# Mixing stage: the last prompt tile's branch products and the picks are placed behind the sample's last tile

## The chip, the cores and the metric

The kernel runs on one core of a Trainium2 chip. The metric is the device time of one execution in microseconds (us); smaller is better. An execution is one launch that computes both outputs, the prompt's 256 rows and the sample's 1024 rows.

## The reference

An encoder layer on two sequences of 256 and 1024 tokens, 1024 wide: input norm, one wide projection, neighbourhood attention (8 heads) beside a gated linear recurrence (4 heads, both directions), a gated mix of the two branches, a norm, and an expert-choice feed-forward layer with 16 experts. What the change touches is the mix, the router and the choice of tokens:

```python
a_out = a_out.reshape(B, T, NA_WIDTH) @ w_branch_na[l]
r_out = (o_hg * jax.nn.silu(g_hg)) @ w_branch_hg[l]
mix = jax.nn.sigmoid(gate_na) * a_out + jax.nn.sigmoid(gate_hg) * r_out
x = layer_norm(ALPHA * x + mix @ w_out[l], ln1_g[l], ln1_b[l])
...
cap = EC_FACTOR * n_tok // N_EXPERTS
aff = jax.nn.softmax((xf @ w_router).astype(jnp.float32), axis=-1)
gate, idx = lax.top_k(aff.T, cap)
xs = xf[idx]
hdn = jax.nn.silu(jnp.einsum('ecd,edf->ecf', xs, w_gate)) * jnp.einsum('ecd,edf->ecf', xs, w_up)
out = jnp.einsum('ecf,efd->ecd', hdn, w_down) * gate[..., None].astype(x.dtype)
```

Each expert takes its 32 best prompt tokens and its 128 best sample tokens. The whole layer runs once for the prompt and once for the sample.

## The kernel before

The kernel is one program of stages, written engine by engine: each engine (PE for matmuls, DVE, ACT, POOL, and SP, which issues loads) has its own instruction list in the order in which the code issues it, and semaphores join them. Nothing is scheduled by a tool: the order on each engine is the order of the calls. A stage ends at a barrier of all engines.

**The mixing stage** (`stage_mix_out`, L1504) works on 10 tiles of 128 tokens, in an order `MIX_ORDER` that takes the 8 sample tiles first (t = 0 to 7) and the 2 prompt tiles last (t = 8 and 9). For each tile t the steps, with the names that the code and this text use, are:

- `turn_oh`, `copy_oh`, `o_low`: the recurrence's normed output is transposed on PE (4 transposes, L1717), copied by ACT as the high part and split by DVE into its low part.
- `mix(t, x)`, x = 0, 1: the branch products, 24 matmuls of 512 columns for each half x of the output columns, 12 for each branch (L1736 to L1738); `weigh` (DVE, L2039) multiplies each by its gate, `add` (POOL, L1959) adds the two branches into `mixt`.
- `turn_mix`, `copy_mix`, `m_low`: 8 transposes on PE, the high part on ACT, the low part on DVE (L2045).
- `out(t, x)`: the output projection, 24 matmuls for each half (L1755 to L1757); `add_up` (DVE, L2053 and L2056) adds the residual and takes the statistics, `gather_stats`, `invert` (POOL), `centre` (L2066) and `shift` (L2076) do the norm.
- `turn_x1`, `copy_x1`, `logits`: 8 transposes and 8 small router products (L1770, 16 columns wide), then `find_max` (DVE, L2081), `exp` (ACT, L1894), `normalise` (DVE), `turn_aff` (one transpose on PE, L1775) and `keep` (DVE, L2104), which puts the tile's router weights into the table `affT`.

PSUM gives the transposes two buffers, `tp[0]` and `tp[1]`, used in turn in the order of the list `units`: a transpose waits (`wait_bank`) until the low part of the one two places ahead in that list has been taken. In a steady turn of the loop, PE does `turn_aff(t-2)`, `turn_oh(t+1)`, `mix(t+1, 0)`, `turn_mix(t)`, `mix(t+1, 1)`, `turn_x1(t-1)`, `out(t, 0)`, `logits(t-1)`, `out(t, 1)`.

**The picks.** DVE finds each expert's best tokens in rounds of three instructions over `affT` (`pick`, L1492: the 8 largest, their positions, their removal; L1498, L1500, L1501), so 47 picks for 128 tokens. As soon as the 8 sample tiles are in `affT`, the first `EARLY_PICKS` = 24 of them run on DVE in the mixing stage, in gaps between the work of tiles 8 and 9. The others run at the start of the expert stage. The prompt's rows of `affT` can take part only when tile 9 is in; its 4 rounds are the `JOINT_ROUNDS` 8 to 11, where one instruction works on sample rows and prompt rows together (80 rows and not 48).

**The start of the expert stage** (`stage_experts`, L2226). DVE: picks 24 to 35 (the joint ones), pick 36, `find_prompt`, pick 37, `list_prompt` (the prompt's lists, L2888 and on, which wait for a transpose on PE), picks 38 to 46, `list_sample` (writes `pair`, waits for PE to turn it, then writes the list of the sample's tokens, L2897 to L2916). POOL: gathers the prompt's rows once `list_prompt` is there and the sample's rows once `list_sample` is. PE, in this order: `turn_prompt_lists`, 28 transposes that keep it busy (`warm`, L2639), `turn_in_prompt` (the gathered prompt rows), then `session(0)`, 128 prompt products (L2559); the transposes of the sample's lists are called inside that session, ahead of its fourth piece of weights:

```python
for m in range(SESSION):
    g = SESSION * n + m
    if g == 3:
        turn_sample_lists()
    pe.wait_ge(w_ready[g % RAW], 16 * (g // RAW + 1))
```

Each piece has 16 products, so that 48 stand ahead of them. After the session come the sample's gathered rows, transposed and split, and then 16 experts' matmuls without a pause worth the name.

## Time and profile before

| | us |
|---|---|
| median of 3 runs | 2694.84 |
| lowest and highest run | 2692.8, 2696.47 |
| the profiled execution, its own time | 2697.44 |
| its span, first to last instruction | 2695.7 |

The profiled execution is 2.6 us above the median of the runs. PE is busy for 97% of the span, and TensorE's granted clock has a mean of 0.986 of full speed. In the rows further down, a line of a timeline or of the chain of waits begins with the start in us from the span's start and the duration in us; what stands in square brackets is the idle time of the engine ahead of it and what ended it. A count (x4) says that several instructions are merged. In the table by windows each engine has its busy time in us and its instructions; then come the granted clock of TensorE, the busy share of the DMA engines and GB/s. The length that a PE row shows includes its drain: from start to start the 512-column matmuls stand 0.23 us apart.

### The profile page before, as it was taken

To read this page: it belongs to the slowest core of one execution; us is meant where nothing else is said; L and a number is where in the kernel's file an instruction comes from. 1 tells how busy PE (TensorE), PEld (TensorE's weight loads), DVE (VectorE), ACT (ScalarE), POOL (GpSimd) and SP (SyncE) were. 2 spreads that over 40 slices of the span, in tenths; PEclk is the share of its full clock that TensorE was granted. 3 is DMA by queue.
4 is the path that set the end of the run, shared out by engine and by line. 5 is a ranking of instruction groups with operands and counts; after the bars stand their busy time and mean duration, and the time that the engine had idled before them with its cause. 6 is when DMAs were issued, how large, how long until landed. Compare 5 with 4: busy or idle time off the path is not lost.

```text
span 2695.7 us, 44888 instructions
## 1 busy us (share of the span) xinstructions
PE 2617.9 (97%) x18504; PEld 2079.8 (77%) x18504; DVE 1673.8 (62%) x2091; ACT 1370.4 (51%) x1800; POOL 507.0 (19%) x454
## 2 busy tenths in 40 slices
PE   9999999999999999969999999999999999999997
PEld 7888888777778788857777777777777777777775
DVE  7212220875654566576777667776777667776887
ACT  3111220866664434325566656665566656666674
POOL 2211120123332234310110010001001100111444
PEclk9999999999999999979999999999999999999999
DMA  7567783676666743366778877888788878888983
GB/s 252 172 197 211 242 276 125 240 292 215 215 239 225 257 156 125 118 244 237 281 289 294 313 276 282 293 313 290 267 304 303 289 286 304 301 286 329 342 337 128
DMA packets 238347, 683.59 MB, mean 254 GB/s; under 512 B 20081, under 2 KB 66680, under 8 KB 233024
## 3 DMA queue, kind: packets, MB, share of 16 engines
q1 hardware_dynamic: 220608, 630.58, 64.8%
q0 software_dynamic: 17536, 50.14, 6.6%
q8 instruction: 147, 2.41, 0.4%
q14 instruction: 56, 0.46, 0.0%
HBM read 576.67 MB, written 103.95 MB: 252 GB/s over the span
## 4 chain that ended last, share of the span: by engine, by line
PE 52%; DVE 1%; POOL 1%; issue 0%; ACT 0%; DMA 0%; ACTq 0%; POOLq 0%; DVEq 0%
PE moe_strip L2559 12%; PE moe_up L2574 4%; PE moe_down L2574 4%; PE moe_down L2576 4%; PE moe_up L2575 4%; PE moe_down L2575 4%; PE moe_up L2576 4%; PE moe_gate L2574 4%; PE moe_gate L2576 4%; PE moe_gate L2575 4%; PE moe_up L2496 1%; PE moe_turn L2532 1%; PE moe_gate L2507 0%; ACT pieces_high L2682 0%; POOL moe_minus_mean L2378 0%
## 5 line engine op out<-in xcount | busy, mean ns | idle before, releaser
L2790 DVE TENSOR_TENSOR pieces_low<-pieces_raw,pieces_high 128x1024 fp32r<-128x1024 f32 x768 | 893.6, 1219 | 349.9 <-PE moe_strip L2559 336.6
L2682 ACT ACTIVATE pieces_high<-pieces_raw 128x1024 fp32r<-128x1024 f32 x768 | 769.5, 1051 | 333.9 <-PE moe_up L2576 196.6
L2559 PE MATMUL moe_strip<-pieces_raw,pieces_xT_p 128*32 128x256 f32 x4096 | 227.9, 380 | 0.5 <-ACT pieces_xT_p L2694 0.5
L2574 PE MATMUL moe_gate<-pieces_high,pieces_xT 128*128 128x512 f32 x512 | 202.4, 395 | 1.5 <-DVE pieces_low L2790 0.8
L2574 PE MATMUL moe_up<-pieces_high,pieces_xT 128*128 128x512 f32 x512 | 202.9, 396 | 0.0
L2574 PE MATMUL moe_down<-pieces_high,pieces_hdn 128*128 128x512 f32 x512 | 202.8, 396 | 0.0
L2559 PEld LDWEIGHTS moe_strip<-pieces_raw,pieces_xT_p 128*32 128x32 f32 x4096 | 129.7, 110 | 93.8 <-issue 10.9
L2576 PE MATMUL moe_gate<-pieces_low,pieces_xT 128*128 128x512 f32 x512 | 199.6, 390 | 0.0
L2575 PE MATMUL moe_up<-pieces_high,pieces_xT 128*128 128x512 f32 x512 | 199.6, 390 | 0.0
L2575 PE MATMUL moe_gate<-pieces_high,pieces_xT 128*128 128x512 f32 x512 | 199.5, 390 | 0.0
L2576 PE MATMUL moe_down<-pieces_low,pieces_hdn 128*128 128x512 f32 x512 | 199.5, 390 | 0.0
L2575 PE MATMUL moe_down<-pieces_high,pieces_hdn 128*128 128x512 f32 x512 | 199.4, 389 | 0.0
L2576 PE MATMUL moe_up<-pieces_low,pieces_xT 128*128 128x512 f32 x512 | 199.1, 389 | 0.0
L2336 POOL COPY moe_at_in<-main_picks 32x1 uint32<-32x1 uint32 (+1 forms) x30 | 21.5, 744 | 768.9 <-PE moe_up L2496 764.3
L526 DVE COPY fr_out<-fr_acc 128x512 f32<-128x512 f32 (+1 forms) x28 | 17.7, 634 | 176.5 <-PE fr_acc L385 102.1
L1153 PE MATMUL hg_facc<-bias_fw,bias_fx 128*128 128x512 f32 x288 | 120.1, 417 | 5.6 <-PEq L103 2.1
L2574 PEld LDWEIGHTS moe_up<-pieces_high,pieces_xT 128*128 128x128 f32 x512 | 96.1, 188 | 32.3 <-issue 13.2
L2574 PEld LDWEIGHTS moe_down<-pieces_high,pieces_hdn 128*128 128x128 f32 x512 | 96.1, 188 | 25.8 <-issue 6.6
L1154 PE MATMUL hg_facc<-bias_fw,bias_fx 128*128 128x512 f32 x288 | 115.2, 400 | 0.0
L1155 PE MATMUL hg_facc<-bias_fw,bias_fx 128*128 128x512 f32 x288 | 114.9, 399 | 0.0
L2559 PE MATMUL moe_strip<-pieces_raw,moe_hdn_p 128*32 128x256 f32 x2048 | 113.8, 380 | 0.0
L2574 PEld LDWEIGHTS moe_gate<-pieces_high,pieces_xT 128*128 128x128 f32 x512 | 96.2, 188 | 21.8 <-DVE pieces_low L2790 1.9
(386 smaller groups left out, 5328.5 us busy)
## 6 DMA issues: line engine op xcount, KB each, us to landing
pieces_raw<-in_w_gate_e SPq DMA_DIRECT2D x128, 1024.0 KB, 5.3
pieces_raw<-in_w_up_e SPq DMA_DIRECT2D x128, 1024.0 KB, 7.3
pieces_raw<-in_w_down_e SPq DMA_DIRECT2D x128, 1024.0 KB, 5.0
bias_fx<-xs SPq DMA_DIRECT2D x40, 1024.0 KB, 5.3
fr_raw<-in_w_in SPq DMA_DIRECT2D x16, 1024.0 KB, 9.4
ws<-fr_late_split SPq DMA_DIRECT2D x32, 512.0 KB, 4.4
bias_fw<-ws SPq DMA_DIRECT2D x32, 512.0 KB, 9.0
mo_gates<-h SPq DMA_DIRECT2D x20, 512.0 KB, 4.4
```

The costliest lines, as they stand in the source:

```text
L1153: nc.tensor.matmul(f_acc[i % 2][:], fx[:, i % 2, 0, c, :], hi, start=(c == 0), stop=False)
L1154: nc.tensor.matmul(f_acc[i % 2][:], fx[:, i % 2, 0, c, :], lo, start=False, stop=False)
L1155: last = nc.tensor.matmul(f_acc[i % 2][:], fx[:, i % 2, 1, c, :], hi, start=False, stop=(c == KD - 1))
L2336: nc.gpsimd.tensor_copy(to[n][:], picks[n][:, e:e + 1]).then_inc(at_ready, 1)
L2496: last = nc.tensor.transpose(to[:, k * P:(k + 1) * P], rows_s[:, (4 * j + k) * P:(4 * j + k + 1) * P], ident[:])
L2532: last = nc.tensor.transpose(hidden_turned(c)[:, k * P:(k + 1) * P], hid[:, c % 2, k * P:(k + 1) * P], ident[:])
L2559: last = nc.tensor.matmul(strip_ps[j * CP:(j + 1) * CP, kind, :], x, raw[g % RAW][:, k * D + j * STRIP:k * D + (j + 1) * STRIP], start=sta ...
L2574: nc.tensor.matmul(to[:], x_k[:, kk, 0:CS], hi, start=(kk == 0), stop=False)
L2575: nc.tensor.matmul(to[:], x_k[:, kk, CS:2 * CS], hi, start=False, stop=False)
L2576: return nc.tensor.matmul(to[:], x_k[:, kk, 0:CS], lo, start=False, stop=(kk == count - 1))
L2682: nc.scalar.activation(high[:, g % HI, cols], raw[g % RAW][:, cols], ACT.Copy).then_inc(hi_done, 1)
L2790: nc.vector.tensor_tensor(low[g % RAW][:, cols], raw[g % RAW][:, cols], high[:, g % HI, cols].bitcast(F32), ALU.subtract).then_inc(lo_done, 1)
```

## The change

Only the mixing stage's orders and two constants are touched. The amount of work is the same: the same instructions run, with the same shapes, except that which pick stands in which stage changes. The steady loop now runs for t = 0 to 6, and from tile 7 (`Z`) on the order is written out for each engine. `mix(9, ...)`, the branch products of the last prompt tile, stand behind `logits(7)` and not ahead of `turn_x1(7)`. 33 picks run in the mixing stage in place of 24, and the joint rounds are 11 to 14 in place of 8 to 11, so that `find_prompt` and `list_prompt` follow picks 45 and 46, the last two. Nothing in `stage_experts` is edited.

```diff
-SAMPLE_TILES, EARLY_PICKS = SEQS[1][1] // P, 24
-JOINT_ROUNDS = range(8, 8 + CAPS[0] // 8)
+SAMPLE_TILES, EARLY_PICKS = SEQS[1][1] // P, 33
+JOINT_ROUNDS = range(11, 11 + CAPS[0] // 8)
...
+        units += [("mix", Z, 0), ("mix", Z, 1), ("oh", Z + 1, 0)]
+        units += [("x1", t, n) for t in (Z - 1, Z) for n in range(2)]
+        units += [("oh", Z + 2, 0)]
+        units += [(kind, t, n) for kind in ("mix", "x1") for t in (Z + 1, Z + 2) for n in range(2)]
...
+                turn_aff(Z - 2)
+                turn_mix(Z)
+                turn_oh(Z + 1)
+                mix(Z + 1, 0)
+                out(Z, 0)
+                turn_x1(Z - 1)
+                out(Z, 1)
+                logits(Z - 1)
+                mix(Z + 1, 1)
+                turn_aff(Z - 1)
+                turn_x1(Z)
+                turn_oh(Z + 2)
+                logits(Z)
+                mix(Z + 2, 0, (0,))
+                turn_aff(Z)
+                mix(Z + 2, 0, (1,))
+                turn_mix(Z + 1)
+                mix(Z + 2, 1)
+                out(Z + 1, 0)
+                out(Z + 1, 1)
+                turn_mix(Z + 2)
+                out(Z + 2, 0)
+                turn_x1(Z + 1)
+                out(Z + 2, 1)
+                logits(Z + 1)
+                turn_aff(Z + 1)
+                turn_x1(Z + 2)
+                logits(Z + 2)
+                turn_aff(Z + 2)
...
+                copy_x1(Z)
+                copy_oh(Z + 2)
+                open_gates(Z + 2, (0,))
+                exp(Z)
+                scale(Z)
+                open_gates(Z + 2, (1,))
...
+                invert(Z)
+                add(Z + 1, 1)
+                store(Z)
+                add(Z + 2, 0)
+                add(Z + 2, 1)
...
+                add_up(Z - 1, 1)
+                gather_stats(Z - 1)
+                m_low(Z)
+                o_low(Z + 1)
...
+                keep(Z)
+                pick_sample(0, 1)
...
+                pick_sample(12, 18)
+                add_up(Z + 1, 1)
+                gather_stats(Z + 1)
+                centre(Z + 1)
+                m_low(Z + 2)
+                shift(Z + 1)
+                pick_sample(18, 23)
+                add_up(Z + 2, 0)
+                pick_sample(23, 28)
+                find_max(Z + 1)
+                add_up(Z + 2, 1)
+                gather_stats(Z + 2)
+                centre(Z + 2)
+                normalise(Z + 1)
+                shift(Z + 2)
+                keep(Z + 1)
+                pick_sample(28, 31)
+                find_max(Z + 2)
+                pick_sample(31, 32)
+                normalise(Z + 2)
+                pick_sample(32, EARLY_PICKS)
+                keep(Z + 2)
```

The orders at three places follow, before and after. `mo_acc_out` is `out`'s accumulator, `mo_small` the router's, `mo_tp` the two transpose buffers, `mo_acc` the accumulators of `mix`.

PE where tile 7 begins, behind `out(6, 1)`, before:

```order
L1757 MATMUL mo_acc_out<-mo_wo_hi,mo_m_lo 128x512
L1775 MATMUL mo_small<-main_ident,mo_aff 80x128
L1717 MATMUL mo_tp<-main_ident,mo_oh 128x128 x4
L1736 MATMUL mo_acc<-mo_wb_hi,mo_act_hi 128x512
L1737 MATMUL mo_acc<-mo_wb_lo,mo_act_hi 128x512
```

and now:

```order
L1761 MATMUL mo_acc_out<-mo_wo_hi,mo_m_lo 128x512
L1779 MATMUL mo_small<-main_ident,mo_aff 80x128
L1723 MATMUL mo_tp<-main_ident,mo_mixt 128x128 x8
L1723 MATMUL mo_tp<-main_ident,mo_oh 128x128 x4
L1742 MATMUL mo_acc<-mo_wb_hi,mo_act_hi 128x512
```

The 8 transposes of `turn_mix(7)` moved from behind `mix(8, 0)` to ahead of `turn_oh(8)`, and fill both transpose buffers there.

DVE from the last picks ahead of `add_up(8, 1)` to `shift(8)`, before:

```order
L1498 MAX route_best<-main_affT 48x8
L1500 MAX_INDEX route_at<-route_best,main_affT 48x8
L2053 SCALAR_TENSOR_TENSOR wroom<-wroom,mo_acc_out 128x512
L2056 BN_STATS mo_stats<-wroom 128x6
L2060 BN_AGGR mo_mv<-mo_stats 128x2
L2045 TENSOR_TENSOR mo_m_lo<-mo_tp,mo_m_hi 128x512 x2
L2066 SCALAR_TENSOR_TENSOR wroom<-wroom,mo_mv,mo_g_all 128x1024
L2076 SCALAR_TENSOR_TENSOR wroom<-wroom,mo_rstd,mo_b_all 128x1024
```

and now:

```order
L1498 MAX route_best<-main_affT 48x8
L1500 MAX_INDEX route_at<-route_best,main_affT 48x8
L1501 MATCH_REPLACE main_affT<-route_best,main_affT 48x512
L2112 SCALAR_TENSOR_TENSOR wroom<-wroom,mo_acc_out 128x512
L2115 BN_STATS mo_stats<-wroom 128x6
L2119 BN_AGGR mo_mv<-mo_stats 128x2
L2125 SCALAR_TENSOR_TENSOR wroom<-wroom,mo_mv,mo_g_all 128x1024
L2104 TENSOR_TENSOR mo_m_lo<-mo_tp,mo_m_hi 128x512 x2
L2135 SCALAR_TENSOR_TENSOR wroom<-wroom,mo_rstd,mo_b_all 128x1024
```

`m_low(9)` moved behind `centre(8)`; six picks, not five, now stand between `add_up(8, 0)` and `add_up(8, 1)`.

DVE in the expert stage, from the second pick behind the joint ones, before:

```order
L1500 MAX_INDEX route_at<-route_best,main_affT 48x8
L2888 CAST moe_at_in<-moe_up 32x1
L2889 COPY main_gates<-moe_up 32x16
L2890 CAST main_picks<-moe_up 32x16
L2891 COPY main_gates<-moe_up 128x16
L2892 CAST main_picks<-moe_up 128x16
L1501 MATCH_REPLACE main_affT<-route_best,main_affT 48x512
L1498 MAX route_best<-main_affT 48x8
L1500 MAX_INDEX route_at<-route_best,main_affT 48x8
```

and now:

```order
L1500 MAX_INDEX route_at<-route_best,main_affT 48x8
L2968 CAST moe_at_in<-moe_up 32x1
L2969 COPY main_gates<-moe_up 32x16
L2970 CAST main_picks<-moe_up 32x16
L2971 COPY main_gates<-moe_up 128x16
L2972 CAST main_picks<-moe_up 128x16
L2977 COPY moe_pair<-route_best 16x128
L2978 TENSOR_SCALAR moe_pair<-route_at 16x128
```

The nine picks between `list_prompt` and the writing of `pair` are gone from there; ahead of them the same 14 picks stand as before.

## Rows read from the trace of the kernel before

**Rows 1.** Chain of waits, 1197 to 1240 us: start, us, what.

```profile
1209.15 5.07 PE moe_gate L2639 x28
...
1215.30 2.80 PE moe_strip L2559 x48
1218.09 0.27 PE moe_up L2633 x2
...
1219.45 4.30 DMA pieces_rows_s<-x,moe_at_in
...
1226.46 0.50 PE moe_gate L2574
```

**Rows 2.** Timeline of DVE, expert stage: start, us, engine, line, operation.

```profile
1197.85 0.69 DVE L1498 MAX8 route_best<-main_affT 80x8 f32<-80x512 f32 x1
...
1209.49 0.15 DVE L2888 CAST moe_at_in<-moe_up 32x1 uint32<-32x1 f32 x1
...
1217.27 0.21 DVE L2903 TENSOR_SCALAR moe_pair<-route_at 16x128 f32<-16x128 uint32 x1
1218.38 0.19 DVE L2906 COPY moe_taken<-moe_up 128x32 f32<-128x32 f32 x1 [0.90 <-PE moe_up L2633]
```

**Rows 3.** Windows: us; busy PE, PEld, DVE, ACT, POOL; PEclk; DMA.

```profile
1112.00:1138.00 26.00, 26.00 (x135) 21.95 (x134) 16.02 (x23) 9.92 (x14) 9.96 (x10) 1.00 0.32 101
...
1154.00:1159.00 5.00, 5.00 (x18) 4.02 (x19) 0.57 (x3) 0.52 (x3) 0.00 (x0) 0.66 0.96 354
...
1166.00:1175.00 9.00, 7.47 (x38) 6.10 (x37) 8.22 (x15) 2.15 (x3) 1.97 (x4) 1.00 1.03 411
...
1183.00:1187.00 4.00, 0.31 (x3) 0.21 (x2) 3.15 (x7) 0.58 (x3) 1.88 (x2) 0.83 0.00 0
1187.00:1193.00 6.00, 5.63 (x25) 5.23 (x25) 4.94 (x14) 2.04 (x3) 1.16 (x2) 0.50 0.44 175
```

**Rows 4.** Timeline of DVE, then PE, where tile 7 begins.

```profile
1112.97 0.69 DVE L2053 SCALAR_TENSOR_TENSOR wroom<-wroom,mo_acc_out 128x512 f32<-128x512 f32 x1 [4.56 <-PE mo_acc_out L1757]
...
1120.81 1.28 DVE L2045 TENSOR_TENSOR mo_m_lo<-mo_tp,mo_m_hi 128x512 fp32r<-128x512 f32 x2
...
1112.88 0.60 PE L1717 MATMUL mo_tp<-main_ident,mo_oh 128*128 128x128 f32 x4
...
1118.81 1.04 PE L1717 MATMUL mo_tp<-main_ident,mo_mixt 128*128 128x128 f32 x8
```

**Rows 5.** Timeline of DVE, then PE, around the second half of tile 8.

```profile
1161.85 0.69 DVE L2053 SCALAR_TENSOR_TENSOR wroom<-wroom,mo_acc_out 128x512 f32<-128x512 f32 x1 [0.25 <-PE mo_acc_out L1757]
...
1167.22 0.69 DVE L2053 SCALAR_TENSOR_TENSOR wroom<-wroom,mo_acc_out 128x512 f32<-128x512 f32 x1 [0.28 <-PE mo_acc_out L1757]
...
1168.80 1.23 DVE L2045 TENSOR_TENSOR mo_m_lo<-mo_tp,mo_m_hi 128x512 fp32r<-128x512 f32 x2
1169.95 1.27 DVE L2066 SCALAR_TENSOR_TENSOR wroom<-wroom,mo_mv,mo_g_all 128x1024 f32<-128x1024 f32 x1
...
1169.58 0.47 PE L1755 MATMUL mo_acc_out<-mo_wo_hi,mo_m_hi 128*128 128x512 f32 x1 [1.52 <-DVE mo_m_lo L2045]
```

**Rows 6.** Timeline of ACT in a tile of the steady loop.

```profile
1114.13 1.28 ACT L1868 ACT_TABLE_LOAD   x1
1115.42 2.01 ACT L1868 ACTIVATE mo_gates<-mo_gates 128x1024 f32<-128x1024 f32 x2
...
1133.57 0.28 ACT L1894 ACTIVATE mo_aff<-mo_small,mo_nmax 128x16 f32<-128x16 f32 x1 [5.41 <-DVE mo_nmax L2081]
```

**Rows 7.** Timeline of DVE, then PE, at the end of the mixing stage.

```profile
1185.47 1.28 DVE L2076 SCALAR_TENSOR_TENSOR wroom<-wroom,mo_rstd,mo_b_all 128x1024 f32<-128x1024 f32 x1 [0.75 <-issue]
...
1181.46 1.85 PE L1770 MATMUL mo_small<-mo_wr,wroom 128*128 128x16 f32 x16
1187.15 0.43 PE L1775 MATMUL mo_small<-main_ident,mo_aff 128*80 128x128 f32 x1 [3.84 <-DVE mo_aff L2087]
1187.38 1.92 PE L1717 MATMUL mo_tp<-main_ident,wroom 128*128 128x128 f32 x8
```

More of the change, by code:

```diff
@@ L1801, in _, with turn_mix, turn_x1 @@
                 mix(1, 0)
-                for t in range(0, NT + 2):
-                    if 0 <= t - 2 < NT and t - 2 != SAMPLE_TILES - 1:
+                def turn_mix(t):
+                    for n in range(2):
+                        pe.wait_ge(added, 2 * t + n + 1)
+                        turn(("mix", t, n), mixt[:, half_of(n)], m_turned)
+                def turn_x1(t):
+                    pe.wait_ge(x1_done, t + 1)
+                    for n in range(2):
+                        turn(("x1", t, n), x1_sb[:, half_of(n)], x1_turned)
@@ L1825, in _ @@
-                    if t == NT - 1:
-                        out(t, 1)
-                    if 0 <= t - 1 < NT and t != SAMPLE_TILES:
-                        logits(t - 1)
-                    if 0 <= t < NT - 1:
-                        out(t, 1)
+                    turn_mix(t)
+                    mix(t + 1, 1)
+                    if t >= 1:
+                        turn_x1(t - 1)
+                    out(t, 0)
+                    if t >= 1:
+                        logits(t - 1)
+                    out(t, 1)
@@ L1863, in copy_oh, with open_gates @@
                     nc.scalar.activation(act_hi[:, 1], blocks(bank_of(("oh", t, 0))[:]), ACT.Copy).then_inc(o_hi, 1)
-                def open_gates(t):
-                    for x in range(2):
+                def open_gates(t, halves=(0, 1)):
+                    for x in halves:
                         act.wait_ge(gates_in[x], 16 * t + 16)
@@ L2155, in _ @@
[L2155 to L2162 removed]
+                    weigh(t + 1, 1, 0)
+                    prepare(t + 2)
+                    weigh(t + 1, 1, 1)
+                    a_low(t + 2)
+                    norm_heads(t + 2)
@@ L2163, in _ @@
+                    add_up(t, 0)
+                    if t >= 1:
                         find_max(t - 1)
                         normalise(t - 1)
-                t = NT - 1
-                keep(t - 2)
-                pick_sample(0, 3)
-                add_up(t - 1, 0)
-                pick_sample(3, 8)
-                add_up(t - 1, 1)
-                gather_stats(t - 1)
-                m_low(t)
-                centre(t - 1)
-                shift(t - 1)
-                pick_sample(8, 11)
@@ L2177, in _ @@
-                add_up(t, 0)
-                pick_sample(11, 15)
-                add_up(t, 1)
-                gather_stats(t)
-                centre(t)
-                find_max(t - 1)
-                shift(t)
-                normalise(t - 1)
-                keep(t - 1)
-                pick_sample(15, 21)
-                find_max(t)
-                pick_sample(21, 22)
-                normalise(t)
-                pick_sample(22, EARLY_PICKS)
-                keep(t)
+                add_up(Z - 1, 1)
@@ new lines, in _ @@
+                gather_stats(Z - 1)
+                m_low(Z)
+                o_low(Z + 1)
+                centre(Z - 1)
+                keep(Z - 2)
+                shift(Z - 1)
+                weigh(Z + 1, 0, 0)
+                weigh(Z + 1, 0, 1)
+                prepare(Z + 2)
+                add_up(Z, 0)
+                norm_heads(Z + 2)
+                add_up(Z, 1)
+                gather_stats(Z)
+                find_max(Z - 1)
+                centre(Z)
+                normalise(Z - 1)
@@ new lines, in _ @@
+                shift(Z)
+                weigh(Z + 1, 1, 0)
+                weigh(Z + 1, 1, 1)
+                a_low(Z + 2)
+                keep(Z - 1)
+                o_low(Z + 2)
+                find_max(Z)
+                normalise(Z)
+                keep(Z)
+                pick_sample(0, 1)
+                weigh(Z + 2, 0, 0)
+                pick_sample(1, 2)
+                weigh(Z + 2, 0, 1)
+                m_low(Z + 1)
+                pick_sample(2, 5)
+                weigh(Z + 2, 1, 0)
```

120 lines of the change are left out of this document (55 added, 65 removed).

## The prediction, made before the changed kernel was run

> **What bounds the kernel now.** I read the windows first, then the timelines of the mixing stage's last tiles, then the chain of waits across the barrier. In the mixing stage's steady loop PE has no gap: 26.00 us busy in a window of 26.00 us, one tile, at the full clock, with DVE at 16.02 us [rows 3]. So up to tile 7 a step moved on DVE, ACT or POOL costs nothing, and the stage's length is PE's work plus what PE waits for. The places to look at are the waits of the tail, and those that the new order makes. Before, they are 1.52 us for `m_low(9)` [rows 5] and 3.84 us for tile 8's router weights [rows 7].
>
> Across the barrier the chain of waits does not run along the picks to their end. It runs from `list_prompt` to PE: the 28 keep-busy transposes (5.07 us), the prompt's gathered rows, 48 of the session's products (2.80 us), and only then, at 1218.09, the transposes of the sample's lists; from there to the gather of the sample's rows (4.30 us to landing) and the first expert matmul at 1226.46 [rows 1]. DVE writes the last part of `pair` at 1217.27, 0.21 us long, and then sits 0.90 us for PE [rows 2]. From 1226 us on PE is dense again, so whatever delays that matmul delays the end.
>
> **The change, part by part.** The work is the same; only waits can change. Let S be the start of the first pick of the expert stage, 1197.85 before [rows 2]. The end moves by (move of S) plus (change from S to the first expert matmul).
>
> 1. *From S to the first expert matmul: nothing.* Nine picks leave this stretch. One is 0.69 us for the 8 largest [rows 2], some 0.77 us with its gap, so that nine are 6.9 us of DVE. But 14 picks stood ahead of `list_prompt` before (24 to 37) and 14 stand there now (33 to 46), 12 of them joint in both. So `list_prompt` comes at S + 11.64 us (1209.49 − 1197.85, [rows 2]) as before. PE needs from it to the transposes of the sample's lists 1218.09 − 1209.49 = 8.60 us [rows 1, 2] through work that is the same and in the same order. DVE would have `pair` written about 7 us sooner and wait for PE 7.8 us and not 0.90. The gain that the nine picks could give is bounded by the slack that PE had: the lists' transposes began 0.6 us after `pair` was written, because PE was late, so the gain is 0 us; its other end, if PE's queue could let them pass, is 6.9 us (a rival below).
>
> The trace shows PE starting these transposes right behind the 48th product. The Trainium skill states as a rule that only weight loads are pulled ahead in PE's queue and that matmuls stay in program order (TensorE: Matmul & The Clock Gate, "What happens when you issue a matmul"). By that rule this part is 0 us; without it, it could be up to the 6.9 us.
>
> 2. *`turn_mix(7)` ahead of `turn_oh(8)`: +1.6 us.* With both transpose buffers filled by `turn_mix(7)`, `turn_oh(8)` must wait until `m_low` has taken the first. PE finishes `out(6, 1)` at about 1112.8, and 8 transposes end at 1113.7 (0.79 us from the start of the 8 at 1118.81 to the next matmul). DVE does `add_up(6, 1)` from 1112.97, two instructions at 0.72 us each, then 0.2 us of `gather_stats`, then the first half of `m_low(7)`, 0.69 us, so the buffer is free at 1115.3 [rows 4]. Before, `mix(8, 0)` stood in between and hid it all. Bounds: 1.4 (no gaps) to 1.8 us.
>
> 3. *Tile 7's softmax: +0.9 us.* `turn_aff(7)` now stands behind only `logits(7)` and half of `mix(9, 0)`, 1.7 (start to start; 1.85 with the drain, [rows 7]) + 12 × 0.23 = 4.45 us. In that time ACT does `copy_oh(9)` (0.6 us), loads a table (1.28), opens half the gates (1.0, half of 2.01), loads the other table (1.28) and then does `exp` with its read-out (0.46) [rows 6], and DVE the 0.5 us of `normalise`: 5.1 us against 4.45. With 0.15 us more where `logits(7)` waits for `keep(6)` it comes to 0.15 + 0.75. Before, half of `out(8, 0)` and one load covered it. Bounds: 0.4 to 1.3 us.
>
> 4. *`m_low(9)` behind `centre(8)` and one more pick: +1.65 us.* Before, `add_up(8, 1)` started 0.2 us after `out(8, 1)` ended (1167.22) and `m_low(9)` 1.58 us later [rows 5]. Now six picks of 0.77 us follow `add_up(8, 0)`: 0.2 + 1.34 + 4.6 = 6.15 us after the end of `out(8, 0)`, while `out(8, 1)` takes 24 × 0.23 = 5.5 us; `add_up(8, 1)` is 0.65 us late, 0.45 more than before. `centre(8)` adds 1.20 us (1.27 with its tail) [rows 5]. PE's wait grows from 1.52 to about 3.2 us. Bounds: 1.2 (picks not late) to 1.9 us.
>
> 5. *The end of the stage: +0.5 us.* `add_up(9, 1)` now stands behind `find_max(8)`, which waits for `logits(8)`, 1.85 us [rows 7], and takes 0.17: +2.0 us. Against it, `normalise(8)` is ahead of `shift(9)`, so `turn_aff(8)` no longer delays `turn_x1(9)`: it began at 1187.38 though `shift(9)` ended at 1186.7 [rows 7], −0.7 us. And one pick less, two and not three, lies in the last softmax: −0.77 us. Bounds: −0.2 to +1.2 us.
>
> Sum of the waits: 1.6 + 0.9 + 1.65 + 0.5 = 4.65 us, with bounds 2.8 and 6.2.
>
> 6. *The clock: +1.7 us.* Of the waits before, the one of 3.84 us took the granted clock from 2.4 to 1.2 GHz (0.83 in 1183 to 1187, then 0.50), and the one of 1.52 us did not (1.00 in 1166 to 1175). A stretch of transposes, a short wait and 16-column products ahead of `out(8, 0)` did too: 0.66 over 1154 to 1159, which at 5.00 × (1 − 0.66) is 1.7 us of matmul work lost [rows 3]. Now the wait at `m_low(9)` is 3.2 us behind 0.8 us of transposes, nearer to the 3.84 than to the 1.52, and `out(9, 0)` follows it. I take one more fall with the price of that row, 1.7 us; bounds 0 and 3.4 (a second one, behind the wait of part 2 or 3). The light stretch at `logits(7)` stays and I leave its fall as it is; the one at the stage's end is in both.
>
> The Trainium skill states that the slow clock is the default which activity lifts (TensorE: Matmul & The Clock Gate, "Part 1: The HAM clock gate"). The rows at 1183 to 1193 agree with it. By it the sum is 6.35 us if the wait at `m_low(9)` counts as idle for the gate, and 4.65 us if it doesn't.
>
> POOL's new order, ACT's split gates and SP's loads cost nothing. Tile 9's second gates are loaded only once `add(8, 1)` is done, with `x_in` for tile 8 queued behind them on SP, but the gates are needed only after `exp(7)` and `x_in` only at `add_up(8, 0)`, two `mix` halves and an `out` later. The first pieces of expert weights, released by the last `mix`, come about 4 us later and are hidden by all of tiles 8 and 9's `out`. If one were late, it would show as a wait of ACT or DVE of that length.
>
> Total: S and the end move by 4.65 + 1.7 = 6.35 us. The profiled execution was 2697.44 us, so it would be 2703.8; its distance of 2.6 us to the median is kept out, and I put the sum on the median: 2694.84 + 6.35 = 2701.2 us. That is +0.24%. A measurement of this kernel can tell about 0.2%, or 5.4 us, from no change.
>
> **The rivals.**
>
> *The clock stays up at `m_low(9)`* (30%). For it: 1.52 us didn't lower it, and tile 8's delays may give DVE time for its picks and shorten the wait. Then 2694.84 + 4.65 = 2699.5 us, within 0.2%.
>
> *Two more falls* (13%), the second behind `turn_mix(7)` or around tile 7's softmax, where PE's waits now come between transposes: 4.65 + 3.4 = 8.05 us, 2702.9 us.
>
> *The picks pay after all* (7%): the sample's lists are turned when `pair` is ready, DVE having been what PE waited for. For it: the 23 picks fill the chain in front, and the 48th product ended close to the writing of `pair`, 0.6 us after. Against it: DVE's wait of 0.90 us [rows 2]. It decides from the point where PE reaches the transposes ahead of `pair`. The nine picks, 6.9 us, would pay for the waits of 6.35 us: 2694.3 us, not slower.
>
> *The gain is real on PE's side* (3%): if ACT and DVE have more slack in the tail than single durations say and none of parts 2 to 4 shows, 2694.84 + 0.5 = 2695.3 us.
>
> **How the numbers follow.** My forecast, 2701.2 us, has 47%; the rivals have 30, 13, 7 and 3%. The predicted time is the forecast's. The cases spread by another 1 us each for runs. Slower by over 0.2% (above 2700.2) is three quarters of the forecast, all of the case with two falls and a fifth of the first rival: 35 + 13 + 6 = 54%. Faster by over 0.2% (below 2689.5) no case gives; I leave 4% for what I don't see. Within 0.2% is the rest, 42%. The range takes in the first rival with the lower bounds of its waits (2.8 us: 2697.6) less 1.1 us for runs, 2696.5, and above it the two falls and the upper bounds, 2704.5.
>
> **What would show it.** Right: in the new trace PE waits 1.6 us at `turn_oh(8)`, 0.7 at `turn_aff(7)`, about 3.2 for `m_low(9)`; the first 80-row pick starts 5 to 7 us later; from it to the first expert matmul there are 28.6 us as before; DVE waits over 7 us for PE's transposes of `pair`. Wrong: if that last wait is short and the 28.6 us have become 22, part 1 is wrong; if S hasn't moved, parts 2 to 5 are; if the granted clock stays at 1.00 through `out(9, 0)`, part 6 is.

## The result, and the profile of the changed kernel

| | before | changed |
|---|---|---|
| median, us | 2693.32 | 2703.1 |
| lowest and highest of 7 runs each, us | 2692.45, 2697.95 | 2699.5, 2705.65 |
| ratio, changed over before | | 1.0027, 95% interval 1.0017 to 1.0036 |
| the profiled execution, us | 2697.44 | 2701.34 |
| its span, us | 2695.7 | 2699.6 |

The changed kernel is slower by 0.27%. Of the median before, the interval is 4.6 to 9.7 us, and the 6.35 us that the prediction summed lie in it.

The two kernels run the same list on PE up to the small transpose right behind `out(6, 1)`, `turn_aff(5)`. I call its start the **anchor** and measure from it to S, the first 80-row pick of the expert stage, from S to the first expert matmul, and from there to the end:

| us | anchor | anchor to S | S to first expert matmul | from there to the end |
|---|---|---|---|---|
| before | 1112.77 | 85.08 | 28.61 | 1469.24 |
| changed | 1111.28 | 91.60 | 28.66 | 1468.06 |

The mixing stage's tail grew by 6.52 us and the start of the expert stage by nothing. The first and the last stretch hold work that the change doesn't touch; they came out 1.5 and 1.2 us shorter in this execution, which is why its span is only 3.9 us longer. Over the traces of this study the last stretch lies between 1465.7 and 1471.2 us, without regard to the edit; a part of it is PE's wait in the last expert for the prompt's hidden rows, between 0.38 and 2.80 us. It was 1.50 us before and 0.39 in the changed kernel, which is nearly all of the 1.2 us. So the edits are read below from the anchor on, and not from spans.

Windows of the changed kernel: us; busy PE, PEld, DVE, ACT, POOL; PEclk; DMA share; GB/s. They answer to [rows 3].

```profile
1111.00:1137.00 26.00, 24.59 (x127) 20.66 (x127) 16.57 (x26) 9.81 (x14) 9.08 (x11) 1.00 0.19 61
1143.00:1147.00 4.00, 4.00 (x13) 3.06 (x12) 0.40 (x2) 3.95 (x6) 0.12 (x1) 0.57 0.92 294
1169.00:1178.00 9.00, 6.62 (x17) 5.27 (x18) 7.49 (x14) 1.06 (x1) 3.06 (x4) 0.62 1.02 391
...
1191.00:1197.00 6.00, 4.23 (x18) 3.64 (x19) 3.99 (x9) 2.25 (x3) 1.84 (x4) 0.50 0.38 152
```

Tile 7's stretch, dense before, now has 1.4 us without a matmul. The light stretch around `logits(7)` drops to half the clock as it did before (0.57 here, 0.66 over 1154 to 1159 in [rows 3]), the stage's end does too, and a third fall is new: 0.62 over 1169 to 1178, where before had 1.00. The waits behind it stand in PE's timeline (start, duration, idle time ahead in brackets); its first line is the anchor:

```profile
1111.28 0.27 PE L1779 MATMUL mo_small<-main_ident,mo_aff 128*80 128x128 f32 x1
1111.38 1.03 PE L1723 MATMUL mo_tp<-main_ident,mo_mixt 128*128 128x128 f32 x8
1113.83 0.63 PE L1723 MATMUL mo_tp<-main_ident,mo_oh 128*128 128x128 f32 x4 [1.42 <-DVE mo_m_lo L2104]
...
1171.38 0.76 PE L1759 MATMUL mo_acc_out<-mo_wo_hi,mo_m_hi 128*128 128x512 f32 x1 [3.29 <-DVE mo_m_lo L2104]
...
1191.39 0.43 PE L1779 MATMUL mo_small<-main_ident,mo_aff 128*80 128x128 f32 x1 [3.49 <-DVE mo_aff L2146]
1193.21 1.97 PE L1723 MATMUL mo_tp<-main_ident,wroom 128*128 128x128 f32 x8 [1.38 <-DVE wroom L2135]
```

The wait at `turn_oh(8)`, 1.42 us, didn't exist; the one for `m_low(9)` was 1.52 [rows 5] and is 3.29; at the end 3.84 us [rows 7] have become 3.49 and 1.38. DVE shows why `m_low(9)` is late (first fence line: `add_up(8, 1)`, without idle time ahead, so the sixth pick reached into it), and what the nine picks left behind:

```profile
1167.67 0.67 DVE L2112 SCALAR_TENSOR_TENSOR wroom<-wroom,mo_acc_out 128x512 f32<-128x512 f32 x1
1168.37 0.69 DVE L2115 BATCH_NORM_STATS2 mo_stats<-wroom 128x6 f32<-128x512 f32 x1
1169.10 0.21 DVE L2119 BATCH_NORM_AGGREGATE mo_mv<-mo_stats 128x2 f32<-128x12 f32 x1
1169.35 1.28 DVE L2125 SCALAR_TENSOR_TENSOR wroom<-wroom,mo_mv,mo_g_all 128x1024 f32<-128x1024 f32 x1
1170.55 1.28 DVE L2104 TENSOR_TENSOR mo_m_lo<-mo_tp,mo_m_hi 128x512 fp32r<-128x512 f32 x2
...
1202.88 0.63 DVE L1498 MAX8 route_best<-main_affT 80x8 f32<-80x512 f32 x1
...
1223.51 0.19 DVE L2986 COPY moe_taken<-moe_up 128x32 f32<-128x32 f32 x1 [7.86 <-PE moe_up L2713]
```

And the chain of waits across the barrier (start, us, what), against [rows 1]:

```profile
1214.10 5.25 PE moe_gate L2719 x28
...
1220.43 2.80 PE moe_strip L2639 x48
1223.22 0.27 PE moe_up L2713 x2
...
1224.58 4.25 DMA pieces_rows_s<-x,moe_at_in
...
1231.54 0.50 PE moe_gate L2654
```

It is the same chain, 5.1 us later. DVE now waits 7.86 us and not 0.90 [rows 2] for PE's transposes of `pair`, 7 us longer: the nine picks' time went into that wait.

### The profile page after: what moved, and what is told of

It reads as the page before. It is cut to its first block, busy times and chain, and to the rows that moved or that the text cites. A ratio compares the mean times of both kernels' runs of the same rounds, so it can differ in the third digit from the quotient of the medians.

```text
span 2699.6 us, 44889 instructions
## 1 busy us (share of the span) xinstructions
PE 2619.7 (97%) x18504; PEld 2080.1 (77%) x18504; DVE 1672.8 (62%) x2091; ACT 1372.3 (51%) x1802; POOL 499.5 (19%) x454
## 4 chain that ended last, share of the span: by engine, by line
PE 50%; DMA 1%; DVE 1%; POOL 1%; issue 1%; ACT 1%; POOLq 0%; ACTq 0%; DVEq 0%
PE moe_strip L2639 12%; PE moe_up L2654 4%; PE moe_up L2655 4%; PE moe_up L2656 4%; PE moe_gate L2654 4%; PE moe_gate L2656 4%; PE moe_gate L2655 4%; PE moe_down L2654 4%; PE moe_down L2656 4%; PE moe_down L2655 4%; DMA out<-moe_norm_x 1%; POOL moe_minus_mean L2458 1%; PE moe_up L2576 0%; DVE pieces_low L2870 0%; PE moe_turn L2612 0%
```

## The experiments

All are edits of the changed kernel. The ratios are against runs of the kernel before on the same chip: median 2695.9 us for e1 to e4, 2695.66 for e9 to e11. "Fall A" is the fall of the granted clock right behind the light stretch at `logits(7)`: the 12 matmuls there take 4.42 or 4.43 us with it and 2.83 to 2.99 us, a wait left out, without it. "Fall B" is the one over `out(9, 0)`, whose 24 matmuls take 8.27 to 8.35 us with it (7.19 in e6) and 5.53 to 5.55 us without.

| kernel | anchor to S | S to first expert matmul | fall A | fall B | us, median | ratio to before, 95% |
|---|---|---|---|---|---|---|
| before | 85.08 | 28.61 | yes | no | | |
| changed | 91.60 | 28.66 | yes | yes | 2703.1 | 1.0027 (1.0017 to 1.0036) |
| e1_nine_back | 88.83 | 28.14 | yes | no | 2701.32 | 1.0021 (1.0011 to 1.0031) |
| e2_m_low_first | 87.07 | 29.06 | yes | no | 2699.45 | 1.0008 (0.9998 to 1.0018) |
| e3_filled_wait | 88.86 | 28.28 | yes | no | 2698.04 | 1.0008 (0.9999 to 1.0018) |
| e4_all_undone | 85.75 | 28.10 | yes | no | 2696.98 | 1.0001 (0.9991 to 1.0010) |
| e5_turn_mix_back | 91.35 | 28.75 | yes | yes | one run | |
| e6_split_mix | 88.18 | 28.78 | no | yes, short | one run | |
| e7_end_back | 90.28 | 29.15 | yes | yes | one run | |
| e8_changed_again | 90.91 | 28.73 | no | yes | one run | |
| e9_lists_early | 91.59 | 27.49 | yes | yes | 2699.83 | 1.0011 (1.0002 to 1.0020) |
| e10_all_undone_early | 82.83 | 28.32 | no | no | 2692.69 | 0.9989 (0.9980 to 0.9998) |
| e11_end_filled_too | 80.65 | 27.91 | no | no | 2689.36 | 0.9979 (0.9970 to 0.9988) |
| e12_eighteen_back | 91.66 | 31.80 | yes | yes | one run | |

**Part 1: do nine picks more or less matter?** e1 puts nine instructions of a pick's length back on DVE ahead of the writing of `pair`.

```diff
+                dve.wait_ge(chosen, PICKS - EARLY_PICKS)
+                for n in range(9):
+                    nc.vector.max(strips[0:SAMPLE_ROWS, 8 * n:8 * n + 8], affT[0:SAMPLE_ROWS, :])
                 list_sample()
```

> The changed kernel with nine more DVE instructions (each the 8-largest search of a pick over 48 rows, into an unused tile) between `list_prompt` and the writing of `pair`, about 6.5 us of DVE work where nine picks stood before. If PE, not DVE, sets when the sample's lists are turned, the first expert matmul stays 28.7 us behind the first joint pick, DVE's wait for PE shrinks from 7.9 us to about 1.4, and the time stays at that of the changed kernel (within 0.1%). If the picks had been on the path, the 28.7 us become about 35 and the time grows by 6.5 us.

Timeline of DVE in e1:

```profile
1214.45 5.42 DVE L3012 MAX8 moe_strips<-main_affT 48x8 f32<-48x512 f32 x9
...
1222.60 0.19 DVE L2986 COPY moe_taken<-moe_up 128x32 f32<-128x32 f32 x1 [2.08 <-PE moe_up L2713]
```

Another 5.42 us of DVE work shortened its wait from 7.86 to 2.08 us, and S to the first expert matmul stayed (28.14). Over the nine traces that have this stretch unedited (before, changed, e2 to e8) it lies between 28.10 and 29.15 us, so nothing under 1 us can be read from one trace. The nine are free on DVE, whether there or not. e1 also showed something that I hadn't asked: the wait of 3.29 us ahead of `out(9, 0)` is there, but the clock stays at 1.00, and S is 2.77 us sooner than in the changed kernel, which has the same mixing stage. PE in e1, and the window (columns as above):

```profile
1173.75 0.47 PE L1759 MATMUL mo_acc_out<-mo_wo_hi,mo_m_hi 128*128 128x512 f32 x1 [3.29 <-DVE mo_m_lo L2104]
```

```profile
1172.00:1180.00 8.00, 6.25 (x31) 5.28 (x32) 7.37 (x13) 1.14 (x2) 2.83 (x4) 1.00 1.02 397
```

e12 puts 18 back, to find where DVE becomes the bound.

> The changed kernel with 18 more DVE instructions of the picks' length ahead of the writing of `pair` (with nine, DVE's wait was 2.08 us and the first expert matmul at S + 28.1). Theory: PE's slack is 7.9 us, so of 18 x 0.70 = 12.6 us 7.9 are free and 4.7 are paid: S + 33.4, DVE without a wait. Rival: the stretch is bound by DVE or the gather somewhere already, and it grows by 12.6 us or by what DVE adds beyond nine, 6.3: S + 34.4 or more.

Timeline of DVE, then PE, in e12:

```profile
1216.68 10.76 DVE L3012 MAX8 moe_strips<-main_affT 48x8 f32<-48x512 f32 x18
...
1228.50 0.19 DVE L2986 COPY moe_taken<-moe_up 128x32 f32<-128x32 f32 x1 [0.41 <-PE moe_up L2713]
...
1228.14 0.32 PE L2713 MATMUL moe_up<-main_ident,moe_pair 48*128 48x48 f32 x2 [3.09 <-DVE moe_pair L2983]
```

Now PE waits, 3.09 us, and S to the first expert matmul is 31.80, 3.1 us more. I had expected 33.4 because I took 0.70 us for each of the 18; merged they take 10.76 / 18 = 0.60. With that length the sum nearly closes: of DVE's 7.86 us, 0.41 (what it still waits in e12) are the transposes themselves, 7.45 are slack, and 10.76 less 7.45 is 3.3, against the 3.1 paid. The crossing point that the rival "the picks pay after all" needed lies 7.45 us of DVE work away.

**Part 4 and part 6: `m_low(9)` and the clock.** e2 puts `m_low(9)` back ahead of `centre(8)` and one pick behind `shift(8)`.

```diff
-                pick_sample(12, 18)
+                pick_sample(12, 17)
...
-                centre(Z + 1)
                 m_low(Z + 2)
+                centre(Z + 1)
                 shift(Z + 1)
-                pick_sample(18, 23)
+                pick_sample(17, 23)
```

> The changed kernel with part 4 alone undone: `m_low(9)` ahead of `centre(8)`, and five picks and not six ahead of `add_up(8, 1)`. If these two set PE's wait there, it falls from 3.29 us to about 1.6 and the stage's end comes 1.7 us sooner; if in addition the slow clock over `out(9, 0)` came from that wait, the granted clock stays at 1.00 there and another 2.7 us go, 4.4 in all. If the clock falls for another reason, only the 1.7 us go. Rival: the wait only moves to `add_up(9, 0)`, and the time stays.

PE in e2:

```profile
1169.56 0.47 PE L1759 MATMUL mo_acc_out<-mo_wo_hi,mo_m_hi 128*128 128x512 f32 x1 [1.52 <-DVE mo_m_lo L2104]
```

The wait is 1.52 us as before and there is no fall B. Against e1, which has none either, S is 1.76 us sooner: that is part 4 by itself.

e3 leaves the order as changed and gives PE 32 transposes that nobody reads in the wait.

```diff
                 turn_mix(Z + 2)
+                for _ in range(32):
+                    nc.tensor.transpose(acc[0][:, 0:P], ident[:], ident[:])
                 out(Z + 2, 0)
```

> The changed kernel with 32 transposes of the identity into a free accumulator behind `turn_mix(9)`, some 3.2 us of PE work inside the wait of 3.29 us for `m_low(9)`; nothing reads them. If PE's idleness there lowers the clock, it stays at 1.00 through `out(9, 0)`, that block takes 5.5 us and not 8.3, and the stage ends 2.7 us sooner with the same wait for DVE. If the fall has another cause, `out(9, 0)` stays at the slow clock and the time stays or grows by the transposes that stick out.

PE in e3, and the window (columns as above):

```profile
1170.15 3.66 PE L1856 MATMUL mo_acc<-main_ident 128*128 128x128 f32 x32
1173.61 0.47 PE L1759 MATMUL mo_acc_out<-mo_wo_hi,mo_m_hi 128*128 128x512 f32 x1
```

```profile
1170.00:1180.00 10.00, 10.00 (x68) 8.98 (x66) 9.26 (x16) 2.28 (x4) 3.06 (x4) 1.00 1.02 400
```

S is at 88.86, where e1 had it with the wait open and the clock up. e3 agrees with the clock as the cause of the 2.8 us, but e1 takes its proof away: the fall can also be missing with the wait open. So e8 profiles the changed kernel a second time, unedited.

> The changed kernel itself, a second profile. Theory: the wait of 3.29 us ahead of `out(9, 0)` is there each time, and the fall of the clock behind it is not: either S lies 91.6 us behind the anchor with `out(9, 0)` over 8 us long, or 88.8 with 5.5 us. Rival: the nine extra picks or the filled wait of the runs before are what kept the clock up, so that the changed kernel itself falls each time: 91.6 again.

Windows of e8, and PE in e8:

```profile
1142.00:1146.00 4.00, 3.70 (x20) 2.86 (x19) 0.81 (x3) 3.96 (x6) 0.23 (x1) 1.00 0.75 171
1170.00:1177.00 7.00, 6.16 (x15) 4.88 (x16) 6.02 (x12) 1.06 (x1) 1.93 (x4) 0.51 1.03 398
```

```profile
1146.35 0.30 PE L1779 MATMUL mo_small<-main_ident,mo_aff 128*80 128x128 f32 x1 [0.65 <-DVE mo_aff L2146]
```

Neither of my two numbers: fall B is there, but fall A is not, and S is at 90.91. Eight traces have the wait of 3.29 us unfilled; fall B follows it in seven, and e1 is the eighth. The five traces in which that wait is 1.52 us (before, e2, e4, e10, e11) have no fall B, nor has e3. Two rivals stay. One is that e1's extra instructions kept the clock up there; against it, they run 40 us behind the place, and e12, with twice as many, has fall B. The other is that e3 met by luck what e1 met, and not by its filling: it is one trace. I take the fall behind an unfilled wait of 3.29 us as likely and not certain, and its price as the one of `out(9, 0)`: 8.31 us from its first matmul to the next transposes in the changed kernel, 5.54 in e1, 2.77 us.

**Part 2: tile 7's transposes.** e5 puts `turn_oh(8)` and `mix(8, 0)` ahead of `turn_mix(7)` again, on all engines (PE's part is shown).

```diff
                 turn_aff(Z - 2)
-                turn_mix(Z)
                 turn_oh(Z + 1)
                 mix(Z + 1, 0)
+                turn_mix(Z)
                 out(Z, 0)
```

> The changed kernel with the order of tile 7's transposes as before (`turn_oh(8)`, `mix(8, 0)`, `turn_mix(7)`, with the matching orders of ACT and DVE); all else as changed. Theory: the wait is not made by the order of the transposes but by `mix(8, 1)` having left the place between `turn_mix(7)` and `out(7, 0)`: the 1.42 us at `turn_oh(8)` go and about 1.07 us come at `out(7, 0)` (as in the kernel with all four orders undone), net -0.2 to -0.35 us from the anchor to `logits(6)`. Rival (my part 2 as written): `mix(8, 0)` ahead of the transposes hides it all, -1.4 us and no new wait.

PE in e5:

```profile
1120.52 0.47 PE L1759 MATMUL mo_acc_out<-mo_wo_hi,mo_m_hi 128*128 128x512 f32 x1 [1.07 <-DVE mo_m_lo L2104]
```

The 1.42 us are gone, but 1.07 come at `out(7, 0)`, and `logits(6)` starts 20.01 us behind the anchor and not 20.27. The order of the transposes is worth 0.26 us. What before had, and both of these lack, is `mix(8, 1)` between `turn_mix(7)` and `out(7, 0)`. e6 tries that as the cause with the products at hand; its edit is shown against e5:

```diff
                 turn_oh(Z + 1)
-                mix(Z + 1, 0)
+                mix(Z + 1, 0, (0,))
                 turn_mix(Z)
+                mix(Z + 1, 0, (1,))
                 out(Z, 0)
...
                 copy_oh(Z + 1)
-                open_gates(Z + 1)
                 copy_mix(Z)
+                open_gates(Z + 1)
...
+                m_low(Z)
                 weigh(Z + 1, 0, 0)
                 weigh(Z + 1, 0, 1)
-                m_low(Z)
```

> As the run before, but `turn_mix(7)` stands between the two branches of `mix(8, 0)`, 12 matmuls ahead of it and 12 behind (2.7 us each), and `m_low(7)` and `copy_mix(7)` are taken ahead of the weighing and the gates. Theory that any 2.7 us of products between the transposes and `out(7, 0)` cover `m_low(7)`: no wait of PE over 0.1 us from the anchor to `logits(6)`, and `logits(6)` 1.4 us sooner than in the changed kernel (18.8 and not 20.3 us behind the anchor). Rival: ACT, which loads a table and opens gates for 3.3 us there, or DVE's centre and shift are late, and 0.5 us or more of wait comes back at `turn_mix(7)` or `out(7, 0)`.

PE in e6 (the branch products between these rows are left out):

```profile
1112.01 0.60 PE L1723 MATMUL mo_tp<-main_ident,mo_oh 128*128 128x128 f32 x4
...
1115.21 1.04 PE L1723 MATMUL mo_tp<-main_ident,mo_mixt 128*128 128x128 f32 x8
...
1118.82 0.39 PE L1759 MATMUL mo_acc_out<-mo_wo_hi,mo_m_hi 128*128 128x512 f32 x1
```

No wait is left, and `logits(6)` is 18.70 us behind the anchor, exactly where before has it. Twelve products on each side of the transposes cover both chains.

**Part 5: the end of the stage.** e7 puts `add_up(9, 1)` ahead of `find_max(8)` and `shift(9)` ahead of `normalise(8)`.

```diff
                 pick_sample(23, 28)
-                find_max(Z + 1)
                 add_up(Z + 2, 1)
                 gather_stats(Z + 2)
                 centre(Z + 2)
-                normalise(Z + 1)
+                find_max(Z + 1)
                 shift(Z + 2)
+                normalise(Z + 1)
```

> The changed kernel with DVE's order at the end of the stage as before (`add_up(9, 1)` ahead of `find_max(8)`, `shift(9)` ahead of `normalise(8)`). Forecast of part 5: the +2.0 goes and the 0.7 comes back, -1.3 us for the start of the first 80-row pick against a run of the changed kernel with the same clock (88.8 us from the anchor where no fall lies over `out(9, 0)`, 91.6 where one does). From the difference of two earlier runs (87.07 and 85.75, less 0.2 for tile 7) I expect -1.1 us. Rival: `turn_aff(8)` was what PE waited for and `add_up(9, 1)` has slack: 0 us or later.

PE in e7:

```profile
1194.32 0.44 PE L1779 MATMUL mo_small<-main_ident,mo_aff 128*80 128x128 f32 x1 [3.84 <-DVE mo_aff L2146]
```

One wait of 3.84 us, as in [rows 7], in place of 3.49 and 1.38. S is at 90.28; the three traces with the end as changed and both falls have 91.60, 91.59 and 91.66, so the end as changed costs 1.34 us. With the clock up over `out(9, 0)` it is less: from there to S there are 28.74 us in e2, which has the end as changed, and 27.64 in e4 (below), which has it as e7: 1.10 us.

e4 undoes parts 2 to 5 together and keeps only where the tiles and the picks stand: the edits of e2, e5 and e7, and ACT's second gates in one piece.

> The changed kernel with parts 2 to 5 undone and the rest kept: `turn_oh(8)` and `mix(8, 0)` ahead of `turn_mix(7)` again, `exp(7)` ahead of the gates of tile 9 on ACT, `m_low(9)` ahead of `centre(8)` with five picks before `add_up(8, 1)`, `add_up(9, 1)` ahead of `find_max(8)` and `normalise(8)` behind `shift(9)`; 33 picks still run early and `mix(9)` still stands behind `logits(7)`. If the four orders are the whole loss, the time is that of the kernel before within 0.1%, since the nine picks are worth nothing. If moving `mix(9)` or running 33 picks early costs by itself, some us of the loss stay.

PE in e4:

```profile
1119.86 0.47 PE L1759 MATMUL mo_acc_out<-mo_wo_hi,mo_m_hi 128*128 128x512 f32 x1 [1.07 <-DVE mo_m_lo L2103]
...
1187.61 0.44 PE L1779 MATMUL mo_small<-main_ident,mo_aff 128*80 128x128 f32 x1 [4.04 <-DVE mo_aff L2145]
```

S is 0.67 us later than before, and the time is that of before (1.0001). Two moves nearly cancel in it. `logits(6)` comes 1.34 us later than before (20.04 and not 18.70 behind the anchor), behind the wait of 1.07 us that came when `mix(8, 1)` left; from `out(9, 0)` to S there are 27.64 us and not 28.27, with one pick less in the last softmax. So the placing with 33 picks early gives nothing in sum, and the rest of the loss is in the orders around it.

**The lever that the picks needed.** If PE reached the transposes of `pair` sooner, the nine picks should pay. e9 leaves the changed mixing stage alone and moves only the start of the expert stage:

```diff
-                warm(WARM_TURNS[0])
+                warm(12)
+                turn_sample_lists()
+                warm(16)
                 turn_in_prompt(0)
                 session(0)
-                turn_in(0, 0)
-                turn_in(0, 1)
...
-                        if g == 3:
-                            turn_sample_lists()
+                        if g == 4:
+                            turn_in(0, 0)
+                            turn_in(0, 1)
...
                 x_prompt(0)
-                silu_prompt(0, 0)
                 for j in range(2):
                     x_high(0, j)
+                silu_prompt(0, 0)
...
                 list_sample()
-                split(0, (0,))
                 for j in range(2):
                     x_low(0, j)
+                split(0, (0,))
```

> The changed kernel, its mixing stage untouched, with the transposes of `pair` on PE taken out of the session and put behind 12 of the 28 keep-busy transposes, the sample rows' transposes put into the session ahead of its fifth piece, and ACT and DVE taking their copies ahead of the session's results. Theory: the nine picks didn't pay because PE reached the transposes of `pair` late; so the wait of 7.9 us on DVE becomes 1 us or less and the first expert matmul comes at S + 26 and not S + 28.7 (the session's end at S + 25, then one split of 1.2 us): -2.5 us. Rival: something else is late there (the pieces of weights, the prompt rows, ACT), and S + 28 or more stays.

PE, then DVE, in e9:

```profile
1217.80 0.45 PE L2714 MATMUL moe_up<-main_ident,moe_pair 48*128 48x48 f32 x2
...
1221.68 3.66 PE L2640 MATMUL moe_strip<-pieces_raw,pieces_xT_p 128*32 128x256 f32 x64 [0.47 <-ACT pieces_xT_p L2775]
1225.27 1.09 PE L2576 MATMUL moe_down<-main_ident,pieces_rows_s 128*128 128x128 f32 x8
1226.29 3.66 PE L2640 MATMUL moe_strip<-pieces_raw,pieces_xT_p 128*32 128x256 f32 x64
1229.89 1.09 PE L2720 MATMUL moe_gate<-main_ident 128*128 128x128 f32 x8
...
1218.28 0.19 DVE L2987 COPY moe_taken<-moe_up 128x32 f32<-128x32 f32 x1 [1.61 <-PE moe_up L2714]
```

DVE waits 1.61 us and not 7.86, and PE has no wait for the sample's rows any more. But the first expert matmul is at S + 27.49: 1.17 us sooner than in the changed kernel, where I expected 2.5. The eight transposes of the sample's rows now lie inside the session and lengthen it (1.02 us from their start to the next product), which my sum left out; behind the session PE still waits 0.41 us for a split of DVE. From 1214.67 on, where the prompt's lists reach PE, the only other wait in its timeline is the one of 0.47 us for ACT. So PE's own work in this stretch is the bound. The three traces with the early lists have 27.49 (e9), 28.32 (e10) and 27.91 us (e11), against a mean of 28.7 over the nine unedited ones (28.10 to 29.15): of the 6.9 us that the nine picks could give, some 0.8 are to be had by this order, and the scatter is as large.

**A faster kernel.** e10 joins e4, the split of e6 and the early lists of e9.

> The kernel with the picks of the change, the four orders undone (m_low(9) first, the end of the stage and ACT's gates as before), `turn_mix(7)` between the two branches of `mix(8, 0)`, and the sample's lists early as in the run before. Theory: 0.67 us more than before in the mixing stage with the old order of tile 7, less 1.1 to 1.5 for the split, less 2.5 for the lists: 3 to 3.5 us faster than the kernel before, ratio 0.9988. Rival: the expert stage is bound by its weight pieces over its whole length and takes the start's gain back, ratio 0.9997 or more.

Windows of e10 (columns as above):

```profile
1140.00:1147.00 7.00, 7.00 (x40) 5.99 (x40) 3.51 (x9) 5.20 (x7) 1.61 (x3) 1.00 0.74 230
...
1185.00:1190.00 5.00, 5.00 (x24) 4.70 (x23) 2.41 (x6) 1.73 (x3) 0.91 (x2) 0.50 0.53 210
```

The ratio is 0.9989, with an interval that ends just under 1. S is 2.92 us sooner than in e4: the split accounts for 1.34 (`logits(6)` at 18.70 and not 20.04) and the missing fall A for 1.59 (2.84 us for the 12 matmuls and not 4.43); in this execution the first expert matmul came at S + 28.32, so that the early lists show nothing there. Which of these carries the gain of the 11 timed runs isn't told apart. That fall A is missing here need not be luck: all three traces with `mix(8, 0)` split (e6, e10, e11) lack it, and of the ten without the split only e8 does. No run isolates whether the split, or the wait at tile 7 that it removes, prevents the fall.

e11 adds 34 unread transposes ahead of `turn_aff(8)`.

```diff
                 logits(Z + 1)
+                for _ in range(34):
+                    nc.tensor.transpose(acc[0][:, 0:P], ident[:], ident[:])
                 turn_aff(Z + 1)
```

> As the run before, with 34 transposes that nobody reads on PE in the wait of 3.8 us ahead of `turn_aff(8)` at the stage's end. Theory: they keep the clock at 2.4 GHz over `turn_x1(9)` and `logits(9)`, which take 1.84 and 3.57 us there at 1.2 GHz and 0.79 and 1.85 at 2.4: 2.8 us more gained, 6 us in all against the kernel before, ratio 0.9977. Rival: the clock falls all the same (34 transposes don't count, or the fall is set by what comes later), and the transposes delay `turn_aff(8)`: nothing gained or 0.5 us lost against the run before.

PE in e11, and a window:

```profile
1181.41 3.91 PE L1861 MATMUL mo_acc<-main_ident 128*128 128x128 f32 x34
1185.59 0.31 PE L1779 MATMUL mo_small<-main_ident,mo_aff 128*80 128x128 f32 x1 [0.27 <-DVE mo_aff L2148]
1185.73 1.04 PE L1723 MATMUL mo_tp<-main_ident,wroom 128*128 128x128 f32 x8
1187.11 1.95 PE L1774 MATMUL mo_small<-mo_wr,wroom 128*128 128x16 f32 x16 [0.34 <-ACT wroom L1920]
```

```profile
1185.00:1188.00 3.00, 2.39 (x21) 1.95 (x19) 2.46 (x9) 2.14 (x3) 1.16 (x2) 1.00 0.45 177
```

The clock is 1.00 where e10 has 0.50. `turn_x1(9)` and `logits(9)` take 1.04 and 1.95 us, against 1.92 and 3.57 in e10; These are 2.50 us less, and 0.34 us of wait for ACT appear between the two, so that S is 2.18 us sooner than in e10 and not 2.8. In the 13 other traces `turn_x1(9)` takes 1.84 to 1.90 us from its start to `logits(9)`, against 1.38 here with the wait, so that this fall is not one that comes and goes. The early lists and the split are in e10 too. The ratio is 0.9979: 2689.36 us, faster than both kernels.

## Why the prediction was right, point by point

The forecast was 2701.2 us, slower, with a range of 2696.5 to 2704.5; the median is 2703.1. The mechanism, waits in the tail that nine free picks can't pay for, holds. Of its parts, the second had half of its reason wrong, the third didn't appear and the sixth was mis-sized.

- **Part 1, 0 us: right.** S to the first expert matmul is 28.66 us (28.6 forecast), DVE's wait 7.86 us (7.8 forecast). e1 and e12 show the slack, and e9 that PE's place for the transposes of `pair` was what hid the picks, though only some 0.8 of the 6.9 us come back with it.
- **Part 2, +1.6 us: size right, reason half wrong.** PE waits 1.42 us at `turn_oh(8)`, and `logits(6)` starts 20.27 us behind the anchor and not 18.70, 1.57 more. The step that failed is "before, `mix(8, 0)` stood in between and hid it all": with it put back (e5) only 0.26 us return. What hid `m_low(7)` was `mix(8, 1)`, which the new order spends elsewhere; e6 shows that half of `mix(8, 0)` does as well.
- **Part 3, +0.9 us: not in this execution.** PE didn't wait at `turn_aff(7)`, since fall A slowed the 12 products ahead of it: with the clock up, in e8, the wait is 0.65 us. The wait and the fall don't add. With the fall, the 12 products take 4.42 us and not 2.99; with the wait, 0.65; the difference of 0.7 to 0.8 us is the distance of 90.91 to 91.60. I had costed the wait at the full clock and left the fall as it was, though both are at the same place. Before, fall A cost as much (4.43 us for 12 matmuls of `out(8, 0)`), so it adds nothing to the difference. The prediction put 0.75, a slip: its own terms, 5.1 against 4.45 us, give 0.65. The 0.15 us that it added at `logits(7)` appear nowhere; PE waits 0.34 us for ACT ahead of it, as before.
- **Part 4, +1.65 us: right.** The wait is 3.29 us (3.2 forecast), 1.77 more; 1.76 from e1 to e2.
- **Part 5, +0.5 us: right as far as the runs can tell.** The two edits on DVE's order were put at +2.0 − 0.7 = +1.3; e7 measured 1.34. Without fall B it is 1.10 (e2 against e4). The pick less in the last softmax was put at −0.77; e4, whose end is as before but for that, has 0.63 us less from `out(9, 0)` to S. In sum, from `out(9, 0)` to S there are 28.73 us in e1 and 28.27 before: +0.46.
- **Part 6, +1.7 us: place right, size wrong.** The fall came over `out(9, 0)` and cost 2.77 us. The term that was mis-sized is the price taken from the stretch of 0.66 over 1154 to 1159 [rows 3], some 3.4 us at half the clock. Behind a wait on which PE does nothing it was 5.5 us at half the clock (2.77 us lost are 5.54 us at 0.50). In the seven traces the fall had about that length in all but e6, where 1.65 us were lost.

So the waits came to 3.75 us and not 4.65, the clock to 2.77 and not 1.7, and the sum to 6.52 and not 6.35: two misses of about 1 us, of opposite sign. That the sum came within 0.2 us is luck; that it is slower by some us is not. The rival that the clock stays up has been seen once, in e1: anchor to S is 88.83 there, 3.75 us over before, where the rival said 4.65.

What stays open: the medians differ by 9.8 us and the traces by 6.5 from the anchor to the first expert matmul. e1, whose mixing stage is the same, measured 1.0021 (3.0 to 8.4 us), and e8 alone 2700.98 us. That the rest is the scatter of the stretches outside the change fits these numbers, but it wasn't isolated.

## What to carry to other kernels

Before work is moved off an engine, find who the next consumer on the chain waits for: here DVE had only 0.90 us of wait in the profile, and yet nine picks less were worth nothing, because PE came to that point on its own time. A block of matmuls that is moved takes its cover with it; list for each place that it leaves which chain it hid (`mix(8, 1)` hid `m_low(7)`), and split the block if two chains need cover. A wait on PE is priced with the matmuls behind it (here 3.29 us brought a fall of the clock in seven of eight traces, 1.52 us in none of five), and unread transposes in it can be cheaper than the fall: e11's 34 gave 2.18 us. Profile the unchanged kernel a second time before a difference of 3 us is put down to an edit.
